# One 2 MB chunk of expert weights loaded in nine transfers, by partitions, in place of one

## What is computed

```
h   = rms_norm(x, g_mix_norm);  proj = h @ w_in            # 1024 x 7168
x   = x + mixers(proj) @ w_out                             # retention and pooling, gated and merged
h2  = rms_norm(x, g_ffn_norm);  logits = h2 @ w_router + b_router
top-4 of 32 experts per token, softmax over the four
for each expert e and each token routed to it:
    gate, up = split(h2 @ w_gate_up[e] + b_gate_up[e])     # w_gate_up[e]: 1024 x 2048
    act = (clip(up) + 1) * (min(gate, 7) * sigmoid(1.702 * gate))
    y  += weight * (act @ w_down[e] + b_down[e])           # w_down[e]: 1024 x 1024
x   = x + sigmoid(rms_norm(x + y) @ w_ple_gate) * (p @ w_ple_proj)
out = rms_norm(x, g_final)
```

## Time and profile before

| | |
|---|---|
| median of 3 runs | 1223.81 us (1223.16 to 1223.88) |
| profiled execution, its span | 1221.4 us |
| what the median has beyond that span | 2.4 us |
| PE busy | 1143.5 us, 94% of the span |
| DVE / ACT busy | 392.4 us (32%) / 202.4 us (17%) |
| DMA moved | 457.25 MB, mean 374 GB/s |
| chain that ended last | PE 62%, DMA 33%, DVE 3% |

### The profile page before, as it was taken

One profiled execution on the slowest core, in us unless ns is written; L12 is line 12 of the kernel. 1 busy time (PEld: TensorE's weight loads), 2 busy tenths in 40 slices (PEclk: granted clock), 3 DMA queues, 4 the chain that ended last, 5 costly groups with the idle time before them and its releaser, 6 DMA issues.

```text
span 1221.4 us, 12440 instructions
## 1 busy us (share of the span) xinstructions
PE 1143.5 (94%) x5360; PEld 588.4 (48%) x5361; DVE 392.4 (32%) x619; ACT 202.4 (17%) x273; POOL 8.4 (1%) x19
## 2 busy tenths in 40 slices
PE   7999999999999999989898988989999779989887
PEld 6788888874344343424342434343443344343336
DVE  6964765641132121303030403131302121221226
ACT  6464545430000010101010101010100000000115
POOL 0000010000000000000000000000000000000000
PEclk9999999999999999999999999999999989999999
DMA  9855345898999999999999999999999999999990
GB/s 346 317 173 170 114 168 206 357 427 367 399 420 427 428 428 428 428 429 428 427 427 428 428 423 428 428 427 427 427 428 428 429 425 427 427 429 425 421 372 35
DMA packets 57500, 457.25 MB, mean 374 GB/s; under 512 B 5466, under 2 KB 6874, under 8 KB 30370
## 3 DMA queue, kind: packets, MB, share of 16 engines
q1 hardware_dynamic: 55632, 453.26, 89.7%
q10 hardware_dynamic: 1810, 3.14, 0.8%
HBM read 455.34 MB, written 1.05 MB: 374 GB/s over the span
## 4 chain that ended last, share of the span: by engine, by line
PE 62%; DMA 33%; DVE 3%; issue 1%; ACT 0%; SPq 0%; DVEq 0%; ACTq 0%; POOLq 0%; POOL 0%
PE ps L674 61%; DMA ring<-in_w_down 27%; DMA ring<-in_w_gate_up 5%; DVE w_split L1481 1%; PE ps L681 1%; PE ps L982 0%; DMA const<-in_const 0%; PE ps L999 0%; DVE over_xn L1489 0%; SPq L627 0%; DVE ring L1773 0%; DVE ring L1536 0%; DVE B L1719 0%; DVE B L1723 0%; DVE B L1720 0%
## 5 line engine op out<-in xcount | busy, mean ns | idle before, releaser
L674 PE MATMUL ps<-ring,B 128*64 128x512 f32 (+1 forms) x2976 | 659.4, 597 | 50.3 <-DMA ring<-in_w_gate_up 34.2
L674 PEld LDWEIGHTS ps<-ring,B 128*64 128x64 f32 (+1 forms) x2976 | 226.7, 140 | 468.3 <-issue 463.7
L1719 DVE TENSOR_SCALAR B<-ps 128x1024 f32<-128x1024 f32 x16 | 19.6, 1225 | 462.1 <-PE ps L982 379.7
L674 PE MATMUL ps<-w_split,over_BhT 128*128 128x512 f32 x480 | 152.3, 393 | 0.9 <-DVE ring L1540 0.8
L1481 DVE TENSOR_TENSOR w_split<-ring,w_split 128x1024 fp32r<-128x1024 f32 x87 | 104.7, 1223 | 67.8 <-ACT w_split L1224 67.3
L1224 ACT CAST w_split<-ring 128x1024 fp32r<-128x1024 f32 x87 | 90.4, 1052 | 101.6 <-PE ps L674 99.0
L674 PE MATMUL ps<-w_split,over_xn 128*128 128x512 f32 x256 | 100.0, 390 | 0.0
L674 PEld LDWEIGHTS ps<-w_split,over_BhT 128*128 128x128 f32 x480 | 90.0, 189 | 19.9 <-DVE ring L1540 1.2
L1350 ACT COPY B<-ps 128x512 f32<-128x512 f32 x28 | 15.0, 588 | 508.4 <-PE ps L982 508.4
L674 PE MATMUL ps<-const,xn 128*128 128x128 f32 x512 | 61.6, 279 | 4.1 <-DVE const L1688 3.6
L674 PEld LDWEIGHTS ps<-const,xn 128*128 128x128 f32 x512 | 60.0, 196 | 6.8 <-issue 6.8
(11 more groups left out here) (166 smaller groups left out, 495.4 us busy)
## 6 DMA issues: line engine op xcount, KB each, us to landing
ring<-in_w_gate_up SPq DMA_DIRECT2D x118, 2048.0 KB, 32.4
ring<-in_w_down SPq DMA_DIRECT2D x56, 2048.0 KB, 31.8
ring<-in_w_in SPq DMA_DIRECT2D x28, 1024.0 KB, 5.4
ring<-in_w_gate_up SPq DMA_DIRECT2D x18, 1024.0 KB, 11.5
ring<-in_w_down SPq DMA_DIRECT2D x16, 1024.0 KB, 25.5
ring<-in_w_branch SPq DMA_DIRECT2D x8, 1024.0 KB, 6.9
ring<-in_w_out SPq DMA_DIRECT2D x4, 1024.0 KB, 5.0
ring<-in_w_ple_gate SPq DMA_DIRECT2D x4, 1024.0 KB, 19.9
```

Source lines behind the costliest of these rows:

```text
L674: return pe.matmul(out, lhsT, rhs, start=start, stop=stop, skip_group_check=True)
L1719: step(ve.tensor_scalar(gate, two_banks(0), LIMIT, None, ALU.min))
```

## The change

One chunk, number 96, is loaded in nine transfers instead of one, all issued by SP, one after the other, behind the same single wait. The first fills partitions 0 to 63 (1 MB), the other eight fill partitions 64 to 71, 72 to 79 and so on to 127 (128 KB each). The bytes, their places in SBUF and their source addresses stay the same. Each of the nine adds 16 to the place's semaphore; the Ring counts eight more (P // 2 // EIGHT) for that place from then on, so PE waits for all nine. All other chunks are loaded as before.

```diff
@@ -66,6 +66,8 @@
 PLE_RAW = (4, 5, 16, 17)
 LAST_DOWN = (0, 1, 2, 3, 12, 13, 14, 15)
 MORE_PLACES = PLACES - 1
+IN_EIGHTS = 8 * PER_TURN
+EIGHT = 8
@@ -85,6 +87,7 @@
             value, at = free.pop(taken)
             had[at] += g < BIGS - DOWNS - 2
+            had[at] += P // 2 // EIGHT if g == IN_EIGHTS else 0
             self.place.append(at)
@@ -541,6 +544,13 @@
+            def load_up_in_eights(at, m, e):
+
+                w = t["w_gate_up"][0, e, UP_ROWS * P * m:UP_ROWS * P * (m + 1), :].rearrange("(p j) n -> p (j n)", j=UP_ROWS)
+                sp.dma_start(place(at)[0:P // 2, :], w[0:P // 2, :]).then_inc(loaded[at], 16)
+                for p in range(P // 2, P, EIGHT):
+                    sp.dma_start(place(at)[p:p + EIGHT, :], w[p:p + EIGHT, :]).then_inc(loaded[at], 16)
+
@@ -551,7 +561,9 @@
                 if g >= len(LATE_PLACES):
                     sp.wait_ge(used, RING.free_at[g])
-                if down:
+                if g == IN_EIGHTS:
+                    load_up_in_eights(RING.place[g], q // 2, 2 * pair + q % 2)
+                elif down:
                     load_down(RING.place[g], q // 2, 2 * pair + q % 2)
                 else:
                     load_up(RING.place[g], q // 2, 2 * pair + q % 2)
```

## The result

The changed kernel takes 1239.34 us (median of 4 runs, 1236.91 to 1241.87) against 1223.63 us (4 runs, 1223.16 to 1223.88): 15.7 us or 1.3% slower, ratio 1.0128 with a 95% interval of 1.0116 to 1.0140. The forecast was 1238 us in a range of 1228 to 1251. The profiled execution is the longest of the four: its span is 1240.1 us, 18.7 over that of before; it was already 1.1 us late before the change (p's load is issued at 693.0 us and not at 691.9).

A forecast was written before the change was run, and what follows sets the result against it. DMA was taken as the bound. First transfer 4.7 us plus eights 9.8 to 18.6, less 4.9, gave 9.6 to 18.4 us; the middle, 14, on a span of 1221.4 plus 2.4 for the median gave 1238 us, range 1228 to 1251.

The forecast's parts named there:

- What bounds the kernel: Around chunk 96, DMA has no time to spare and PE has; anything beyond 4.9 us goes into the end in full.
- SP's nine issues at nothing: Eight more issues on SP take at least 3.4 us, covered by over 30 us of queued work, so costed at nothing.
- The first transfer, 4.7 us: The 1 MB into partitions 0 to 63 runs at 225 GB/s, taking 4.7 us, which all 16 engines pay.
- The b_down row: b_down's load of 128 KB into 32 partitions loses 0.6 us, twice its own size; by it the first transfer takes 7.3 us.
- the b_gate_up row: b_gate_up's two 256 KB loads into 32 partitions drop the rate from 406 to 225 GB/s; the basis for 4.7 us.
- The eights, 14.2 us with the first transfer's price taken off: Eight transfers into 8 partitions each, on eight engines, slowed by the narrow target; priced between never meeting and in step.
- The bounds, 9.8 and 18.6 us: Time for the eight transfers: 9.8 us if their engines never meet, 18.6 us if they go in step.
- lose a little as hosts and end ahead: Engines without eights lose 2.25 us in the first transfer, are spared 2.45 us, lose a little as hosts, set nothing.
- Count alone: Rival 2: only the count of engines matters at chunk 96, 12 packets instead of 8, +2.45 us, 1226.3 us; 10%.
- rival 3: The eights are dealt to different engines in turn or spread over all 16, no narrow effect: 0 to 2.3 us; 5%.
- The lead of some engines: Rival 4, not slower: engines with eights are some 3 us ahead, so the last ones shed 2.45 us, 1223.3 us; 4%.
- rival 1: The eights go as a convoy or arbitration favours ordinary traffic: 18.4 to 30 us, 1242 to 1254 us; 8% beyond 1251.

The follow-up runs named there:

- nine transfers by columns: Changed kernel with chunk 96 cut by columns, one 1 MB and eight 128 KB transfers, each to all 128 partitions: 1224.61 us, ratio 1.0006.
- the halves: Changed kernel with chunk 96 loaded in two transfers of 64 partitions each, no eights: 1231.98 us, ratio 1.0067.
- to spaced partitions: Changed kernel with each of the eights written to 8 partitions four apart, still reading neighbouring rows: 1235.79 us, ratio 1.0096.
- from spaced rows: Changed kernel with the eights reading rows four apart in memory, still writing to 8 neighbouring partitions: 1238.98 us, ratio 1.0119.
- two engines at home: Changed kernel loading only 16 rows of chunk 96, by two engines into partitions they serve in ordinary chunks: 1218.87 us, ratio 0.9957.
- the eights alone: Changed kernel without the first transfer, only the eight transfers of the upper half: 1234.17 us, ratio 1.0085.
- at turn 4: Changed kernel's split moved to turn 4's first w_gate_up chunk: 1237.81 us with the eights, 1231.39 us with two transfers of 64 partitions.
- two engines away: Changed kernel loading only 16 rows of chunk 96, by two engines into partitions that other engines serve in ordinary chunks: 1223.94 us, ratio 1.0002.

## Why the prediction was right, by its steps

- **What bounds the kernel.** Right. DMA had no idle time, and what it lost at one place is in the end of the kernel: seven of the nine kernels in the account agree with their sums within 0.8 us, and in the other two the profiled run lay well above the median. The 15.3 us of slack before chunk 96 were worth nothing.
- **SP's nine issues at nothing.** Right: 3 us of SP's time, and nine transfers by columns cost no measurable time.
- **The first transfer, 4.7 us.** The rate was right (225 GB/s in the halves), the length not. The step that failed is the term of 4.7 us, in which all 16 engines pay for their own 4 packets only. They pay from the moment when the first engine enters to that when the last leaves: with the halves 16 us instead of 9.3, so (8.1 + 4.9) / 2 = 6.5 us for each half and not 4.7. Left out of the change it saves 15.7 - 10.2 = 5.5 us, since it overlaps there with the eights. The b_down row had shown it, twice its own size, and I took the b_gate_up row.
- **The eights, 14.2 us with the first transfer's price taken off.** The target was the right cause and not the source or the count, as the pair to spaced partitions and from spaced rows shows. But it is not that few partitions are slow, at 7 GB/s each: with two engines at home two partitions take 16 KB each in 0.61 us, 27 GB/s each, and nothing slows. What costs is that engines write away from home. The bounds, 9.8 and 18.6 us, held: the eights alone cost 10.2 us over before, thus 10.2 + 4.9 = 15.1 us. The price in step, 2.33 us for a transfer, is what the packets from 758 to 761 us take (2.36 us and more), so for a few of the eights that bound was real. The reason for a value between them, that engines apart meet less, is not borne out: at turn 4, closer together, the eights cost 13.9 and not over 15.7 us. Of the 6.4 us between halves and eights in turn 4, 2.45 us are the count; the rest is a longer and deeper dip, with nearly all packets from 452 to 466 us at 1.5 to 1.9 us, where with the halves most take some 1.2. How the order of the engines sets the depth is open.
- **The other engines "lose a little as hosts and end ahead".** Wrong as to the little, right as to the end. With two engines away all sixteen took 1.22 us a packet, and in the changed kernel the ordinary chunks behind chunk 96 were slowed as much as the eights. They do end ahead, by being spared 4 packets: the words of chunk 98 are 8.8 us apart, against 3.6 before.
- **The size.** 14 us forecast, 15.7 measured. Part of this closeness is luck: the first transfer was priced too low (by 1.8 us as the halves have it), no time was given to the others' slow-down, and the 14 us are the middle of two bounds, taken for a reason that the runs do not bear out.
- **Rivals.** Count alone (1226.3 us) fell with the halves; it stands as a term of 2.45 us. No narrow effect fell with the dip. No dealing out in turn (rival 3) fell with the 8 completion words of each of the eights and the spread at chunk 97. The lead of some engines is real (the two engines at home, -5.1 us) but was some 3.6 us at most in turn 9, far under what the eights cost. In step (rival 1) came true only for the few us around 760.
- **The profile foretold.** The dip's place and the shift of later rows were right; the dip was longer than foretold (743 to 768.5 for 748 to 765 us). The nine loads had landed at 770.1 us and not at 765. The floor of the dip, 115 GB/s, was lower than the 200 to 300 named, and PE's single wait of 10 us or more did not come: the longest was 5.92 us.

## What to carry to other kernels

In a stream of loads bound by DMA, a load that covers only some partitions can cost more than its bytes. Where its engines write to partitions that others serve in ordinary chunks, it brought everything in flight here to half the rate or less, from the first engine that reached it to the last that left. Fill all 128 partitions, and cut by columns if a chunk must be cut, which cost nothing here. Where few partitions must be filled, choose them so that each engine writes where it always does (here 0, 4, ... 28 in one transfer; it took the dip away, and the time gained for b_down was too small to be told). Look in the trace for a stretch in which the rate falls while the DMA share stays at 1.

## What the runs showed of the hardware that was not expected

- Two of sixteen engines writing away from home brought the whole core from 424 to 209 GB/s, with every packet of every engine at twice its usual time. Why the other twelve slow down is open; no run looked at it.
- Around the two halves the half rate lasts 3 to 7 us longer than their own bytes take (12 to 16 us against 9.3), and ordinary chunks pass in that time.
- In the slow stretch PE's granted clock fell where it had been waiting, to 0.50, the lower of its two levels (1.2 of 2.4 GHz). The 32 matmuls behind the wait of 5.92 us took 9.69 us against 8.78 in the kernel before. Nothing of that reached the end, since PE had to wait for weights again at 774.85 us. The changed kernel, after the wait of 5.92 us:

```profile
750.00:755.00 5.00, 3.90 (x10) 1.40 (x12) 0.00 (x0) 0.00 (x0) 0.00 (x0) 0.50 1.07 200
```
